# Convolution: 15 of the last 128 channels' 31 taps moved from TensorE to VectorE, between the levels of the RWKV inverse

## The chip, the cores and the metric

The program runs on one NeuronCore of a Trainium2 chip. The metric is the device time of one execution in microseconds. Kernels are compared by the median of their runs. TensorE (PE in the profile, its weight loads PEld), VectorE (DVE), ScalarE (ACT), GpSimd (POOL) and SyncE (SP) each work through an instruction list of their own and meet at semaphores.

## The reference

A token block of 256 rows and 1024 columns goes through three layers in float32: a mixer of a convolution and an RWKV recurrence, cross attention and a gated feed-forward; then block attention, a Mamba-2 mixer, and four more gated feed-forwards. The change is in the first mixer:

```python
def conformer_conv(u, conv_w, conv_b, ln_g, ln_b):
    h = u[..., :D_CONV] * jax.nn.sigmoid(u[..., D_CONV:])
    h = lax.conv_general_dilated(
        h, conv_w[:, None, :], window_strides=(1,), padding=[(CONV_WIDTH - 1, 0)],
        dimension_numbers=("NWC", "WIO", "NWC"), feature_group_count=D_CONV) + conv_b
    h = layer_norm(h, ln_g, ln_b)
    return jax.nn.silu(h)
```

`CONV_WIDTH` is 31 and `D_CONV` is 512: each of 512 channels is a causal convolution of its own over 256 tokens. Beside it stands `rwkv7_recurrence`, a scan over tokens for 8 heads of 64, which the kernel computes in chunks of 64 tokens, with the inverse of a unit triangular matrix for each.

## The kernel before

Most of the kernel is a stream of weights: a 1 MB slot comes by DMA, ScalarE rounds it (`w_hi`), VectorE takes the rest (`w_lo`), and TensorE multiplies with both parts. Slots are numbered; `raw_weights` holds three.

Between the 11 slots of the input projection and those of the output projection stands the part that the change touches. Channels lie on partitions, 128 at a time (`c` = 0 to 3), tokens along the free dimension.

The convolution on TensorE. Four copies of the gated input `glu`, shifted by 0 to 3 tokens, come back from a scratch tensor into `shifted[c]`, and the taps come in `tap_rows`, which lies in slots of `raw_weights` that wait for `conv_mm` before they take weights again. One group (`c`, `g`) is four products of 32 channels each, for taps 4g to 4g+3, accumulated in PSUM bank `CONV_BANK`. So there are 32 groups; a group is 4 float32 products in the program and 8 MATMUL records in the profile (L865). `conv_taps(spot)` issues `IN_SPOT[spot]` groups at one of 13 places among the products of the inverse. ScalarE brings each pair of channel blocks out of PSUM with the bias (`conv_out`, L1583) and counts `conv_evac`; TensorE waits for 2 of it and transposes the result (`conv_to_tokens`, L875), for VectorE's layer norm.

The inverse. It is built for two token blocks t = 0, 1 in five levels `lv`. In a level TensorE does, for each t, the product Q (32 records of L849), which ScalarE copies out (L1599); then, for each t, XT and X (32 records each), which VectorE adds in (L2346, L2349), and the next level's Q of that t waits for the first of these. VectorE also masks the next level's left factors (`next_offsets`, L2335). The order on TensorE from level 1 on is: Q(0), Q(1), taps, XT(0), X(0), taps, XT(1), X(1), and then the next level. In level 4 it is: Q(0), Q(1), taps of spot 11, XT(0), `conv_to_tokens`, XT(1), with no X.

The order of all instructions is written out by hand for each engine. The names `late` and `late_taps` are new with the change; `tmp`, whose first 256 columns `late` takes, is idle between the normalisation of kk and the layer norm.

Of the kernel before, what the change touches and what calls it, by code (L numbers as in the profile page):

```python
# [10 lines left out]
ALU = mybir.AluOpType  # L11
# [3 lines left out]
P = 128  # L15
T = 256
# [7 lines left out]
CONV_WIDTH = 31  # L24
# [16 lines left out]
for _name, _count in STREAM:  # L41
# [3 lines left out]


PCOLS = [("gain", 80), ("ssm_norm", 16), ("mu", 14), ("w0", 4), ("a0", 4), ("k_k", 4), ("k_a", 4), ("r_k", 4),
         ("lnx_g", 4), ("lnx_b", 4), ("conv_b", 4), ("ln_g", 4), ("ln_b", 4),
         ("sconv_w", 128), ("sconv_b", 32), ("wa_up", 512), ("g_up", 512), ("w_dt", 256)]

PROWS = [("q_gain", 128), ("k_gain", 128), ("dt_bias", 32), ("a_log", 32),
# [19 lines left out]
def build_program(nc, W, cols, rows, post_gains, consts, x_in, mem_in, pos_in, taps, edges, gated, out):  # L71
    with ExitStack() as ctx:
# [3 lines left out]
        def sem(name):  # L76
            return ctx.enter_context(nc.semaphore(name))
# [8 lines left out]
        tap_rows = [raw[:, 2 * q:2 * q + 2, :].rearrange("p h n -> p (h n)") for q in range(2)]  # L86
# [4 lines left out]
        shifted = [ap[:].bitcast(F32).rearrange("p (j t) -> p j t", j=4) for ap in (g_hi_t, g_lo_t)] \  # L91
# [22 lines left out]
        PS = ctx.enter_context(nc.psum_tensor("PS", [P, 8, 512], F32))  # L114

        def pc(name, i=0, n=1):
            at = PAT[name][0] + i
            return ptab[:, at:at + n]
# [5 lines left out]
        def cn(name, i=0, n=None):  # L124
            at, w = CAT[name]
            n = w if n is None else n
            return ctab[:, at + i:at + i + n]
# [16 lines left out]
        def region(at, words):  # L144
            assert at + words <= ARENA, (at, words)
            return arena[:, at:at + words]
# [9 lines left out]
        conv = region(o, 1024); o += 1024  # L156
        usig = conv
        MEM = region(o, 2048).rearrange("p (t d) -> p t d", t=TT)
        glu = region(o, 1024); o += 1024
# [25 lines left out]
        inv16 = c65(inv65)[:, :, 1:65]  # L185
        mem_squares = region(o - 1024, 2048).rearrange("p (t d) -> p t d", t=TT)
        tmp = region(o, 1024); o += 1024
        tmpb = V_t.rearrange("p t d -> p (t d)")
        CY = glu.rearrange("p (c t) -> p c t", c=4)

# [71 lines left out]
        S = namedtuple("Signals", NAMES)(*[sem(n) for n in NAMES])  # L262
# [4 lines left out]

            eng.wait_ge(S.half_done, LOOP * i + 2 * (FIRST[name] + slot) + 2)

        TAP_GROUPS = [(c, g) for c in range(4) for g in range(8)]  # L270
        IN_SPOT = [3, 2, 3, 3, 3, 2, 3, 3, 3, 3, 2, 2, 0]
        assert sum(IN_SPOT) == len(TAP_GROUPS) and 4 * 8 >= CONV_WIDTH
        CONV_BANK = 4
        X_BANKS = (5, 7)
# [6 lines left out]
        def half_cols(ap, lv, s):  # L281

            return ap.rearrange("p (b s w) -> p b s w", s=2, w=2 << lv)[:, :, s, :]

        def pair_cols(ap, lv):

            return ap.rearrange("p (e b s w) -> p e b s w", e=2, s=2, w=2 << lv)[:, :, :, 1, :]

        def pair_banks(t, lv):

            return PS[:, 2 * t:2 * t + 2, 0:256].rearrange("p e (b s w) -> p e b s w", s=2, w=2 << lv)[:, :, :, 1, :]
# [222 lines left out]
        def _(pe):  # L514
# [235 lines left out]
            for n in range(11):  # L750
# [5 lines left out]
                if n == 2:  # L756
# [3 lines left out]
                    for q, rows_ in enumerate((slice(0, 64), slice(64, 128))):  # L760
                        for c in range(4):
                            at = PAT["wa_up"][0] + c * P
# [3 lines left out]
                if n == 4:  # L766

                    pe.wait_ge(S.a_ready, 1)
                    for c in range(4):
                        last = mm(PS[:, 6 + c // 2, c % 2 * T:(c % 2 + 1) * T], pc("g_up", c * P, P), Q[:, 13, :],  # L770
                                  start=True, stop=True)
                    last.then_inc(S.g_done, 1)
                    pe.wait_ge(S.kksq_ready, 1)
                    for c in range(4):
                        last = mm(PS[32 * c:32 * c + 32, 4, 0:T], cn("pair32"), tmp[:, c * T:(c + 1) * T], start=True,
                                  stop=True)
# [77 lines left out]
            def conv_taps(spot):  # L854

                first = sum(IN_SPOT[:spot])
                for c, g in TAP_GROUPS[first:first + IN_SPOT[spot]]:
                    if c % 2 == 0 and g == 0:
                        pe.wait_ge(S.shifts_loaded, 8 * 16 * (c // 2 + 1))
                        pe.wait_ge(S.aside_loaded, 16 * (c // 2 + 2))  # L860
                        if c:
                            pe.wait_ge(S.conv_evac, 1)
                    for j in range(4):
                        at = ((c % 2 * 8 + g) * 4 + j) * 32
                        last = mm(PS[32 * j:32 * j + 32, CONV_BANK, c % 2 * T + 4 * g:(c % 2 + 1) * T],  # L865
                                  tap_rows[c // 2][:, at:at + 32], shifted[c][:, j, 0:T - 4 * g], start=g == 0, stop=g == 7)
                    if c % 2 and g == 7:
                        last.then_inc(S.conv_mm, 1)

            def conv_to_tokens():  # L870

                pe.wait_ge(S.conv_evac, 2)
                for t in range(TT):
                    for c in range(4):
                        last = nc.tensor.transpose(PS[:, CONV_IN_BANKS[t], c * P:(c + 1) * P],  # L875
                                                   conv[:, c * T + t * P:c * T + (t + 1) * P], ident)
                last.then_inc(S.convT_done, 1)
# [15 lines left out]
            pe.wait_ge(S.tok_ready, 4)  # L893
            grams_of_k_and_r(0)
            conv_taps(0)
            conv_taps(1)
            pe.wait_ge(S.gram_ready, 2)
            grams_of_a(1)
            conv_taps(2)
            grams_of_k_and_r(1)  # L900

# [47 lines left out]
            def state_kv(t):  # L949
                for c, cs in enumerate(pairs):  # L950
                    for g in range(2 * t, min(2 * t + 2, NCK - 1)):
                        mm(PS[:, 4 + g, cs], K_t[half(g), t, cs], V_t[half(g), t, cs], start=c == 0, stop=False)
# [60 lines left out]
                        if c == 3:  # L1013
                            last.then_inc(S.yc_done, 1)

            pe.wait_ge(S.conv_evac, 2)
            state_kv(0)
            pe.wait_ge(S.rounded_ready, 1)
            pe.wait_ge(S.u_ready, 1)
# [28 lines left out]
            for c in range(4):  # L1048
                for t in range(TT):
                    at = c % 2 * T + t * P  # L1050
# [285 lines left out]
            for n in range(8):  # L1336
# [5 lines left out]
                for j in range(2):  # L1342
                    c = (2 * n + j) % KC
# [8 lines left out]
        def _(act):  # L1352
# [163 lines left out]
            for n in range(11):  # L1516
                split(min(2 * n + 4, 23))
                done(act, "w_in", n)
                if n in MIXED:
                    for j in range(2):  # L1520
                        c = MIXED[n] + j
                        last = A(Q[:, c, :], PS[:, n % 4, j * T:(j + 1) * T], ACT.Copy, scale=mu_rest[:, c:c + 1])
                    last.then_inc(S.pin_ready, 1)
                elif n in VALUE_SLOTS:
                    q = VALUE_SLOTS.index(n)
                    A(glu[:, q * 512:(q + 1) * 512], PS[:, n % 4, :], ACT.Copy).then_inc(S.pin_ready, 1)
                else:
                    q = GATE_SLOTS.index(n)
# [50 lines left out]
            def conv_out(q):  # L1579

                act.wait_ge(S.conv_mm, q + 1)
                for c in (2 * q, 2 * q + 1):
                    last = A(conv[:, c * T:(c + 1) * T], PS[:, CONV_BANK, c % 2 * T:(c % 2 + 1) * T], ACT.Identity,  # L1583
                             bias=pc("conv_b", c))
                last.then_inc(S.conv_evac, 1)
# [10 lines left out]
            for lv in range(5):  # L1596
                for t in range(TT):
                    act.wait_ge(S.invq_done, 2 * lv + t + 1)
                    A(pair_cols(Qis[t], lv), pair_banks(t, lv), ACT.Copy).then_inc(S.invq_ready, 1)  # L1599
                    if t and lv < TT:  # L1600
                        act.wait_ge(S.ru_done, lv + 1)
                        A(RU0[:, lv, :], PS[:, 6, :], ACT.Copy).then_inc(S.ru_ready, 1)
                for t in range(TT):
                    if (lv, t) == (1, 0):
                        conv_out(0)
                    if lv < 3:
                        act.wait_ge(S.invx_done, 2 * (2 * lv + t) + 2)
                        q_zeroed(lv + 1, t)
            conv_out(1)
            for t in range(TT):  # L1610
                act.wait_ge(S.u_done, t + 1)
# [112 lines left out]
            for s in range(16):  # L1724
# [5 lines left out]
                ks = slice(s * P, (s + 1) * P)  # L1730
# [73 lines left out]
            for n in range(16):  # L1804
# [3 lines left out]
                for j in range(2):  # L1808
                    c = 2 * n + j
# [144 lines left out]
        def _(dve):  # L1954
            v = nc.vector
            steps = [0]

            def step(ins):

                steps[0] += 1  # L1960
                ins.then_inc(S.dve_step, 1)
                dve.wait_ge(S.dve_step, steps[0])
# [326 lines left out]
            def plus_eye(ap):  # L2289

                return v.tensor_tensor(h8(ap), h8(ap), b8(cn("eye64")), ALU.add)
# [37 lines left out]
            plus_eye(Xis[0]).then_inc(S.inv_ready, 1)  # L2329
            dve.wait_ge(S.gram_ready, 6)  # L2330
            plus_eye(Xis[1]).then_inc(S.inv_ready, 1)
            def next_offsets(lv, t):

                dve.wait_ge(S.invq_done, 2 * lv + t + 1)
                v.tensor_tensor(h8(Loffs[t]), h8(NLs[t]), b8(cn("off", (lv + 2) * 64, 64)), ALU.mult)  # L2335

            for lv in range(4):
                if lv:
                    for t in range(TT):
                        next_offsets(lv, t)  # L2340
                for t in range(TT):
                    if lv == 0:
                        next_offsets(lv, t)
                    dve.wait_ge(S.invx_done, 2 * (2 * lv + t) + 1)
                    part = pair_cols(XiTs[t], lv)
                    v.tensor_tensor(part, part, pair_banks(t, lv), ALU.add).then_inc(S.inv_ready, 1)  # L2346
                    dve.wait_ge(S.invx_done, 2 * (2 * lv + t) + 2)
                    part = half_cols(Xis[t], lv, 0)
                    v.tensor_tensor(part, part, half_cols(PS[:, X_BANKS[t], :], lv, 0), ALU.add).then_inc(S.inv_ready, 1)  # L2349
            for t in range(TT):  # L2350
                dve.wait_ge(S.invx_done, 16 + t + 1)
                part = pair_cols(XiTs[t], 4)
                v.tensor_tensor(part, part, pair_banks(t, 4), ALU.add).then_inc(S.inv_ready, 1)
# [522 lines left out]
```

## Time and profile before

| | before |
|---|---|
| median of 3 runs | 1570.42 us |
| lowest, highest | 1568.79, 1571.0 us |
| the profiled execution | 1571.65 us |
| its span | 1569.6 us |
| its mean granted TensorE clock | 0.999 |
| PE busy, PEld busy | 1544.0 us, 1345.6 us |
| DVE busy, ACT busy | 1101.8 us, 828.9 us |

The span goes from the first to the last instruction of the profile; the time has 2.05 us more around it. A busy PE counts overlapping products once. In the chain, a row "issue" is time in which TensorE had nothing to do and waited for no semaphore or transfer that the profile shows.

### The profile page before, as it was taken

To read this page: it belongs to the slowest core of one execution; us is meant where nothing else is said; L and a number is where in the kernel's file an instruction comes from. 1 tells how busy PE (TensorE), PEld (TensorE's weight loads), DVE (VectorE), ACT (ScalarE), POOL (GpSimd) and SP (SyncE) were. 2 spreads that over 40 slices of the span, in tenths; PEclk is the share of its full clock that TensorE was granted. 3 is DMA by queue.
4 is the path that set the end of the run, shared out by engine and by line. 5 is a ranking of instruction groups with operands and counts; after the bars stand their busy time and mean duration, and the time that the engine had idled before them with its cause. 6 is when DMAs were issued, how large, how long until landed. Compare 5 with 4: busy or idle time off the path is not lost.

```text
span 1569.6 us, 26683 instructions
## 1 busy us (share of the span) xinstructions
PE 1544.0 (98%) x10644; PEld 1345.6 (86%) x10644; DVE 1101.8 (70%) x1379; ACT 828.9 (53%) x1238; POOL 56.1 (4%) x69
## 2 busy tenths in 40 slices
PE   9999999999999999999999999999999998999999
PEld 8977899888888888888888888888889986788887
DVE  4865955776678767677776767766779938576765
ACT  7633755544446444467644446444466659454443
POOL 1000000000000000000000000000001036000000
PEclk9999999999999999999999999999999999999999
DMA  8332543555554545543455454555534540445452
GB/s 304 139 93 84 178 174 123 187 186 199 187 187 162 194 181 191 205 166 135 138 208 190 179 195 167 187 207 189 181 141 165 187 186 29 164 177 195 178 196 107
DMA packets 41156, 268.46 MB, mean 171 GB/s; under 512 B 5232, under 2 KB 8048, under 8 KB 9712
## 3 DMA queue, kind: packets, MB, share of 16 engines
q1 hardware_dynamic: 40368, 264.63, 46.8%
q0 software_dynamic: 704, 2.62, 0.5%
q8 instruction: 63, 1.03, 0.3%
q14 instruction: 21, 0.17, 0.0%
HBM read 265.66 MB, written 1.58 MB: 170 GB/s over the span
## 4 chain that ended last, share of the span: by engine, by line
PE 92%; DVE 3%; ACT 2%; DMA 1%; issue 1%; SPq 0%; DVEq 0%; ACTq 0%
PE PS L633 25%; PE PS L565 15%; PE PS L566 15%; PE PS L567 15%; PE PS L636 13%; PE PS L849 1%; DMA raw_weights<-W 1%; PE PS L865 1%; PE PS L648 1%; PE PS L655 1%; PE PS L649 1%; PE PS L521 1%; DVE w_lo L1971 1%; ACT x_normed L1874 0%; PE PS L733 0%
## 5 line engine op out<-in xcount | busy, mean ns | idle before, releaser
L1971 DVE TENSOR_TENSOR w_lo<-raw_weights,w_hi 128x1024 fp32r<-128x1024 f32 x487 | 590.0, 1229 | 330.9 <-ACT w_hi L1366 329.6
L1366 ACT ACTIVATE w_hi<-raw_weights 128x1024 fp32r<-128x1024 f32 x488 | 506.4, 1055 | 279.0 <-PE PS L567 135.0
L633 PE MATMUL PS<-h_both,w_hi 128*128 128x512 f32 x1680 | 419.9, 392 | 0.0
L633 PEld LDWEIGHTS PS<-h_both,w_hi 128*128 128x128 f32 x1680 | 304.9, 189 | 56.5
L636 PEld LDWEIGHTS PS<-h_both,w_lo 128*128 128x128 f32 x1680 | 229.2, 190 | 16.4
L636 PE MATMUL PS<-h_both,w_lo 128*128 128x256 f32 x1680 | 234.3, 282 | 0.0
L565 PE MATMUL PS<-w_hi,g_hi 128*128 128x512 f32 x440 | 171.8, 390 | 0.0
L566 PE MATMUL PS<-w_lo,g_hi 128*128 128x512 f32 x440 | 171.8, 390 | 0.0
L567 PE MATMUL PS<-w_hi,g_lo 128*128 128x512 f32 x440 | 171.2, 389 | 0.0
L565 PE MATMUL PS<-h_both,w_hi 128*128 128x256 f32 x560 | 161.0, 288 | 2.6 <-DVE h_both L1997 1.4
L566 PE MATMUL PS<-h_both,w_hi 128*128 128x256 f32 x560 | 158.4, 283 | 0.0
L567 PE MATMUL PS<-h_both,w_lo 128*128 128x256 f32 x560 | 158.3, 283 | 0.0
L565 PE MATMUL PS<-w_hi,h_both 128*128 128x512 f32 x352 | 139.9, 397 | 1.7 <-DVE h_both L2749 1.1
L567 PE MATMUL PS<-w_hi,h_both 128*128 128x512 f32 x352 | 137.7, 391 | 0.0
L566 PE MATMUL PS<-w_lo,h_both 128*128 128x512 f32 x352 | 137.6, 391 | 0.0
L1462 ACT ACTIVATE silu_gate<-silu_gate 128x512 f32<-128x512 f32 x55 | 34.7, 632 | 188.8 <-DVE silu_gate L2126 188.8
L565 PEld LDWEIGHTS PS<-h_both,w_hi 128*128 128x128 f32 x560 | 107.1, 191 | 5.8 <-DVE w_lo L1971 3.3
L566 PEld LDWEIGHTS PS<-h_both,w_hi 128*128 128x128 f32 x560 | 107.2, 192 | 0.4 <-issue 0.2
L567 PEld LDWEIGHTS PS<-h_both,w_lo 128*128 128x128 f32 x560 | 107.2, 191 | 0.0
L567 PEld LDWEIGHTS PS<-w_hi,g_lo 128*128 128x128 f32 x440 | 82.6, 188 | 17.6
L565 PEld LDWEIGHTS PS<-w_hi,g_hi 128*128 128x128 f32 x440 | 82.8, 188 | 15.9
L566 PEld LDWEIGHTS PS<-w_lo,g_hi 128*128 128x128 f32 x440 | 82.8, 188 | 15.3
(401 smaller groups left out, 1598.2 us busy)
## 6 DMA issues: line engine op xcount, KB each, us to landing
raw_weights<-W SPq DMA_DIRECT2D x243, 1024.0 KB, 4.8
raw_weights<-taps SPq DMA_DIRECT2D x2, 1024.0 KB, 5.8
post_gain<-post_gains POOLq DMA_DIRECT2D x3, 512.0 KB, 3.9
x_resid<-x SPq DMA_DIRECT2D x2, 512.0 KB, 4.1
raw_weights<-W SPq DMA_DIRECT2D x2, 512.0 KB, 7.1
h_both<-gated SPq DMA_DIRECT2D x8, 128.0 KB, 3.0
arena<-mem POOLq DMA_DIRECT2D x1, 1024.0 KB, 5.5
out<-x_resid SPq DMA_DIRECT2D x2, 512.0 KB, 2.7
```

The source lines that it names most:

```text
L521: return nc.tensor.transpose(PS[:, xT_base(k) + c // 2, at:at + P], X[:, t, c * P:(c + 1) * P], ident)
L565: mm(out, lhs[0], rhs[0], start=start, stop=False)
L566: mm(out, lhs[0], rhs[1], start=False, stop=False)
L567: return mm(out, lhs[1], rhs[0], start=False, stop=stop)
L633: mm(both_out, w_hi[:, slot, c * P:(c + 1) * P], h_both[:, :, c, :], start=c == 0, stop=False)
L636: last = mm(PS[:, bank + j, 0:T], w_lo[:, slot, c * P:(c + 1) * P], h_hi[:, c, :], start=False, stop=c == KC - 1)
L648: mm(PS[:, bank + j, 0:T], w_lo[:, (n + j) % H, cs], h_hi[:, c, :], start=c == 0, stop=False)
L649: mm(PS[:, bank + j, 0:T], w_hi[:, (n + j) % H, cs], h_hi[:, c, :], start=False, stop=c == KC - 1)
L655: last = mm(PS[:, bank + j, T:2 * T], w_hi[:, (n + j) % H, cs], h_lo[:, c, :], start=c == 0, stop=c == KC - 1)
L1366: A(w_hi[:, n % H, :], raw[:, n % (2 * R), :], ACT.Copy).then_inc(S.hi_ready, 1)
L1462: A(sg[:, b % 2, :], sg[:, b % 2, :], ACT.Silu).then_inc(S.silu_ready, 1)
L1971: v.tensor_tensor(w_lo[:, n % H, :], raw[:, n % (2 * R), :], w_hi[:, n % H, :].bitcast(F32), ALU.subtract).then_inc(S.lo_ready, 1)
```

## The change

Channel block c = 3 has 4 groups on TensorE (taps 0 to 15) in place of 8. Taps 16 to 30 are 15 instructions on VectorE, each multiplying `glu` by one tap's weight and adding it to `late`, four after each of the levels 0 to 2 and three after level 3. Each of them waits for the one before (`step`). At the end `late_joined` adds PSUM, bias and `late` on VectorE in two instructions; ScalarE brings out only c = 2 in its second `conv_out`, and the transposes wait for `conv_evac` 3. The 15 columns of weights are added to the table `ptab`.

```diff
-        TAP_GROUPS = [(c, g) for c in range(4) for g in range(8)]
-        IN_SPOT = [3, 2, 3, 3, 3, 2, 3, 3, 3, 3, 2, 2, 0]
+        GROUPS_OF = [8, 8, 8, 4]
+        TAP_GROUPS = [(c, g) for c in range(4) for g in range(GROUPS_OF[c])]
+        IN_SPOT = [3, 2, 3, 3, 3, 2, 2, 2, 2, 2, 2, 2, 0]
...
-                for c in (2 * q, 2 * q + 1):
+                for c in (0, 1) if q == 0 else (2,):
                     last = A(conv[:, c * T:(c + 1) * T], PS[:, CONV_BANK, c % 2 * T:(c % 2 + 1) * T], ACT.Identity,
...
+            def late_taps(ks):
+
+                for k in ks:
+                    weight = pc("late_taps", k - 16)
+                    x = glu[:, 3 * T:4 * T - k]
+                    if k == 16:
+                        dve.wait_ge(S.glu_ready, 2)
+                        step(v.tensor_scalar(late[:, k:T], x, weight, None, ALU.mult))
+                    else:
+                        step(v.scalar_tensor_tensor(late[:, k:T], x, weight, late[:, k:T], ALU.mult, ALU.add))
+
+            def late_joined():
+
+                dve.wait_ge(S.conv_mm, 2)
+                dve.wait_ge(S.conv_evac, 2)
+                v.tensor_scalar(conv[:, 3 * T:3 * T + 16], PS[:, CONV_BANK, T:T + 16], pc("conv_b", 3), None, ALU.add)
+                v.scalar_tensor_tensor(conv[:, 3 * T + 16:4 * T], PS[:, CONV_BANK, T + 16:2 * T], pc("conv_b", 3),
+                                       late[:, 16:T], ALU.add, ALU.add).then_inc(S.conv_evac, 1)
...
                     v.tensor_tensor(part, part, half_cols(PS[:, X_BANKS[t], :], lv, 0), ALU.add).then_inc(S.inv_ready, 1)
+                late_taps(range(16 + 4 * lv, min(20 + 4 * lv, CONV_WIDTH)))
+            late_joined()
```

On TensorE, before, the stretch from level 2's second spot of taps (spot 8) to the transposes; a program row of `x32` is twice as many records in the profile, the last number is the count:

```order
L865 MATMUL PS<-h_both,raw_weights 32x256 x4
L849 MATMUL PS<-arena 64x8x4 x32
L849 MATMUL PS<-arena,silu_gate 64x2x16 x16
L849 MATMUL PS<-arena 64x2x16 x16
L865 MATMUL PS<-h_both,raw_weights 32x252 x4
L865 MATMUL PS<-h_both,raw_weights 32x248 x4
L865 MATMUL PS<-h_both,raw_weights 32x244 x4
L849 MATMUL PS<-silu_gate,arena 64x2x16 x16
L849 MATMUL PS<-arena,silu_gate 64x2x16 x16
```

The same stretch with the change (line numbers are two higher):

```order
L867 MATMUL PS<-h_both,raw_weights 32x236 x4
L851 MATMUL PS<-arena 64x8x4 x32
L851 MATMUL PS<-arena,silu_gate 64x2x16 x16
L851 MATMUL PS<-arena 64x2x16 x16
L867 MATMUL PS<-h_both,raw_weights 32x232 x4
L867 MATMUL PS<-h_both,raw_weights 32x228 x4
L851 MATMUL PS<-silu_gate,arena 64x2x16 x16
L851 MATMUL PS<-arena,silu_gate 64x2x16 x16
```

The spot between Q and XT has two groups where it had three. The same holds for spots 6, 7 and 8, and the spots after them keep their two groups, which are now the last of c = 3 sooner in its tap order.

On VectorE, with the change, from the last addition of level 2 to the transposed inverse's last additions; all `L2343` rows, `L2349` and `L2350` are new:

```order
L2343 SCALAR_TENSOR_TENSOR arena<-arena,ptab 128x229
L2356 TENSOR_TENSOR silu_gate<-arena,ctab 128x512
L2356 TENSOR_TENSOR arena<-arena,ctab 128x512
L2367 TENSOR_TENSOR arena<-arena,PS 128x16x16
L2370 TENSOR_TENSOR arena<-arena,PS 128x16x16
L2343 SCALAR_TENSOR_TENSOR arena<-arena,ptab 128x228
L2343 SCALAR_TENSOR_TENSOR arena<-arena,ptab 128x227
L2343 SCALAR_TENSOR_TENSOR arena<-arena,ptab 128x226
L2349 TENSOR_SCALAR arena<-PS,ptab 128x16
L2350 SCALAR_TENSOR_TENSOR arena<-PS,ptab,arena 128x240
L2376 TENSOR_TENSOR arena<-arena,PS 128x8x32 x2
```

So the taps stand ahead of the masks of the next level, and the join stands ahead of the additions of level 4.

## Rows read from the trace of the kernel before

**Rows 1.** The page: busy time of two engines, and the chain by engine.

```profile
PE 1544.0 (98%) x10644; PEld 1345.6 (86%) x10644; DVE 1101.8 (70%) x1379; ACT 828.9 (53%) x1238; POOL 56.1 (4%) x69
...
PE 92%; DVE 3%; ACT 2%; DMA 1%; issue 1%; SPq 0%; DVEq 0%; ACTq 0%
```

**Rows 2.** The chain by time, 101 to 136 us: start, length, what.

```profile
101.21 0.96 issue
...
105.57 0.42 issue
...
109.75 0.08 issue
...
112.30 1.57 PE PS L849 x63
113.87 1.41 PE PS L865 x24
115.28 1.92 PE PS L849 x89
117.20 0.00 issue
...
119.34 1.52 PE PS L849 x64
...
121.17 0.14 issue
121.31 1.41 PE PS L865 x22
122.72 2.10 PE PS L849 x104
124.83 0.32 issue
...
128.61 0.94 PE PS L865 x16
129.55 2.45 PE PS L849 x127
132.00 1.08 issue
...
133.27 0.96 PE PS L865 x16
...
134.25 0.85 ACT arena L1583 x2
...
135.24 1.06 PE PS L875 x8
```

**Rows 3.** DMA queues, 99 to 134 us: packets, MB, share.

```profile
q8 instruction: 9, 0.15, 1.9%
```

**Rows 4.** VectorE's timeline at level 2: start, length, instruction, idle before it.

```profile
116.85 0.42 DVE L2349 TENSOR_TENSOR arena<-arena,PS 128x256 f32<-128x256 f32 x1 [0.48 <-PE PS L849]
117.58 0.69 DVE L2335 TENSOR_TENSOR silu_gate<-arena,ctab 128x512 f32<-128x512 f32 x1 [0.30 <-PE PS L849]
118.19 0.68 DVE L2335 TENSOR_TENSOR arena<-arena,ctab 128x512 f32<-128x512 f32 x1
120.00 0.42 DVE L2346 TENSOR_TENSOR arena<-arena,PS 128x256 f32<-128x256 f32 x1 [1.13 <-PE PS L849]
```

**Rows 5.** VectorE groups by form: count, busy us, mean ns, idle.

```profile
L2661 DVE SCALAR_TENSOR_TENSOR x_normed<-PS,ptab,x_normed 128x254 f32<-128x254 f32 x32 | 15.4, 481 | 1.1
...
L2569 DVE TENSOR_SCALAR arena<-arena,small 128x256 f32<-128x256 f32 x8 | 2.8, 348 | 0.0
...
L2223 DVE SCALAR_TENSOR_TENSOR arena<-arena,ptab 128x256 f32<-128x256 f32 x4 | 1.7, 482 | 0.0
...
L2642 DVE TENSOR_SCALAR small<-PS 128x64 f32<-128x64 f32 x1 | 0.2, 216 | 0.0
```

More of the change, by code:

```diff
@@ L47 @@
 PCOLS = [("gain", 80), ("ssm_norm", 16), ("mu", 14), ("w0", 4), ("a0", 4), ("k_k", 4), ("k_a", 4), ("r_k", 4),
-         ("lnx_g", 4), ("lnx_b", 4), ("conv_b", 4), ("ln_g", 4), ("ln_b", 4),
+         ("lnx_g", 4), ("lnx_b", 4), ("conv_b", 4), ("ln_g", 4), ("ln_b", 4), ("late_taps", CONV_WIDTH - 16),
          ("sconv_w", 128), ("sconv_b", 32), ("wa_up", 512), ("g_up", 512), ("w_dt", 256)]
@@ L187, in build_program @@
         tmp = region(o, 1024); o += 1024
+        late = tmp[:, 0:T]
         tmpb = V_t.rearrange("p t d -> p (t d)")
@@ L865, in conv_taps @@
                         last = mm(PS[32 * j:32 * j + 32, CONV_BANK, c % 2 * T + 4 * g:(c % 2 + 1) * T],
-                                  tap_rows[c // 2][:, at:at + 32], shifted[c][:, j, 0:T - 4 * g], start=g == 0, stop=g == 7)
-                    if c % 2 and g == 7:
+                                  tap_rows[c // 2][:, at:at + 32], shifted[c][:, j, 0:T - 4 * g], start=g == 0, stop=g == GROUPS_OF[c] - 1)
+                    if c % 2 and g == GROUPS_OF[c] - 1:
                         last.then_inc(S.conv_mm, 1)
             def conv_to_tokens():
-                pe.wait_ge(S.conv_evac, 2)
+                pe.wait_ge(S.conv_evac, 3)
                 for t in range(TT):
@@ L1014, in rows_carried @@
                             last.then_inc(S.yc_done, 1)
-            pe.wait_ge(S.conv_evac, 2)
+            pe.wait_ge(S.conv_evac, 3)
             state_kv(0)
@@ L2856 @@
               "conv_b": col(a["conv_b"][0]), "ln_g": col(a["conv_ln_g"][0]),
-              "ln_b": col(a["conv_ln_b"][0]), "sconv_w": col(a["ssm_conv_w_2"][0].reshape(-1)),
+              "ln_b": col(a["conv_ln_b"][0]), "late_taps": a["conv_w"][0][::-1][16:, 3 * P:].T, "sconv_w": col(a["ssm_conv_w_2"][0].reshape(-1)),
               "sconv_b": col(a["ssm_conv_b_2"][0]), "wa_up": wa, "g_up": a["g_up"][0], "w_dt": wdt}
```

## The prediction

> **What bounds the kernel now.** I read three views in this order: the page for the bound, the chain by time for this stage, then VectorE's timeline for room. The page says TensorE: busy 98% of the span, 92% of the chain [rows 1]. So a microsecond taken from TensorE's list is worth up to a microsecond, and VectorE's work is free as long as nobody waits for it.
>
> In the stage of the change the chain is products and taps, L849 and L865, back to back, but it has holes called "issue" at 101.21, 105.57, 109.75, 117.20 (0.00), 121.17, 124.83 and 132.00 us [rows 2]. The reader should measure from the end of one hole to the end of the next. 102.17, 105.99, 109.83: 3.82 and 3.84 us. 117.20, 121.31, 125.15: 4.11 and 3.84. 125.15 to 133.08 is 7.93, twice 3.97; 109.83 to 117.20 is 7.37, twice 3.69. And between the holes at 121.17 and 124.83 stand 22 + 104 = 126 records of products [rows 2], each with its weight load. In the same 35 us an instruction queue moves 9 packets of 0.15 MB in all, one each 3.9 us [rows 3]. I read this as instruction fetch: about every 128 products a new block of code is needed, and in this stage TensorE runs through its small products as fast as the blocks come.
>
> The Trainium skill ("Runtime: NRT & Kernel Launch", Instruction fetch mechanics) says that an engine's code is refilled in blocks of 16 KiB, 256 instructions, and that crossing a boundary is mostly hidden. The trace agrees on the block (128 products and 128 loads, 0.15 MB over 9 packets) and not on the second point, as the hole of 1.08 us shows. By the page alone no hole comes back; that is a rival below.
>
> **The change part by part.**
>
> *Four groups fewer.* Sixteen records of taps take 0.94 us and 24 take 1.41 [rows 2], so a group of 8 is 0.47 us, and four are 1.88 us. Without the fetch that would be the gain. But a group is only 8 of the 128 products of a block: where the fetch ends the wait, it is worth 8/128 of 3.83 us, or 0.24 us, and four are worth 0.96 us. Which one holds is to be walked through.
>
> I take these lengths from [rows 2]: two groups 0.94; XT and X of one t with the next two Q, 128 records, 2.45 to 2.5; XT and X of the other, 1.52; and a block no shorter than 3.83 us, the commonest distance. From 113.87 to the boundary at 117.20 are 24 + 89 = 113 records, so the boundary before lies some 14 products ahead of 113.87, at 113.5. All this is an estimate from those rows.
> Spot 6 now ends at 113.87 + 0.94 = 114.81. The next boundary is 98 products into the 128 that follow, reached at 116.7, but the code is there only at 113.5 + 3.83 = 117.3. The other 30 take until 117.9. Spot 7, 1.52 us of products and spot 8 end at 117.9 + 0.94 + 1.52 + 0.94 = 121.3, 126 products on: the boundary, with no wait (117.3 + 3.83 = 121.2). The 128 small products that follow need 2.5 us, but their block is followed by the next at 121.3 + 3.83 = 125.1: a hole of 1.3 us. Then spot 9, 1.52 and spot 10 end at 128.5; the 128 products, with a boundary 32 into them at 129.1 and no wait, end at 131.0, and spot 11 at 131.97. Before, spot 11 ended at 133.27 + 0.96 = 134.23. The last taps are 2.26 us earlier. The next boundary is then some 14 products into XT(0), with its code at 129.1 + 3.83 = 132.97; 18 products are left, so XT(0) ends at 133.35.
> In the kernel before, the hole of 1.08 us at 132.00 stood ahead of spot 11 and thus ahead of ScalarE's and TensorE's last steps of the convolution. Now such a hole falls behind the taps, where TensorE has to wait for the convolution anyway. So the two waits lie over each other.
>
> *The join.* ScalarE's two evictions took 0.85 us and the transposes came 0.14 us after [rows 2]. Now one takes about 0.46, then VectorE does 16 columns and 240 columns. No row has a 16-column one; it costs at most the 0.216 us of 64 columns [rows 5], and at least nothing; I take 0.15, near the row, since 16 columns can't save much against 64. The second is 0.48, after the 128x254 form from PSUM [rows 5]. With 0.05 for the semaphore between: 131.97 + 0.02 + 0.46 + 0.05 + 0.15 + 0.48 + 0.14 = 133.27. Alone the join is some 0.3 us longer than before; here it is done as XT(0) ends at 133.35, so I charge nothing. The transposes start at about 133.35 instead of 135.24: 1.9 us earlier. If the cover were gone, the 0.3 us would count.
>
> *Fifteen taps on VectorE.* The first is a multiplication of 240 columns, about 0.35 us; the others are like the 0.482 us of the 256-column one in SBUF [rows 5]. Waiting for the one before, which adds some 0.03, four make about 2.0 us, all together 7.2 us. They stand ahead of the masks. In level 2 before, VectorE ended an addition at 117.27, did the masks by 118.87 and was idle 1.13 us until 120.00 [rows 4]. In the walk above X(1) of level 1 ends at about 116.1, its addition at 116.5, the taps at 118.5, the masks at 119.8, and the additions of XT(0) and X(0) at 120.2 and 120.6. The next Q(0) waits for the first of these; TensorE reaches it after 64 of the 128 products from 121.3, at 122.5. The slack is 2.3 us. XT(1)'s addition comes after 121.9, when VectorE is free. After level 3 only three taps are left, 1.5 us from about 130.7; they end at 132.2, before the join may start at 132.5. So VectorE's taps cost nothing; the cover is TensorE's 64 products and a spot of taps. Queued behind them on VectorE are the masks and additions, and behind `late_joined` the additions of level 4, wanted by TensorE only after the transposes and XT(1).
>
> *The rest.* Fifteen more columns of `ptab` come with a transfer at the start, in the shade of weights: nothing. Weight slots start 2.3 us sooner as `conv_mm` does: nothing, since an earlier load makes nobody wait. TensorE is busy 98% of the span [rows 1], past this stage as in it, so the gain stays. A shift of the code by 64 instructions may put a small hole in or out elsewhere; I take nothing, and 0.4 us either way.
>
> The sum: 1571.65 - 1.9 = 1569.75 us for the profiled execution. This one stood 1.23 us over the median of the runs, 1570.42, so the median should be 1568.5 us. The bounds hang on the length of a block. With 3.69 us (the 7.37 for two) the walk gives a gain of some 2.4 us; with the 4.11 of the longest every block waits, the last boundary comes at 134.0 and the gain is 0.85 us.
>
> **The rivals.**
> *No hole comes back.* If the holes are no rule but leftovers, 1.88 us of taps go and with them 0.14 + 0.32 + 1.08 = 1.54 us of holes, less 0.3 for the join: 3.1 us, 1567.3 us. For it speaks that 117.20 has length 0.00; against it the even distances. The page of the Trainium skill named above, which calls the crossing mostly hidden, would have it so.
> *The fetch takes all.* Blocks of over 4 us, as the one of 4.11 and the two of 3.97, and the join bare on the path: a gain of 0.85 less 0.3, about 0.5 us, 1569.9 us. For it: two of four late distances are that long. Against it: in those TensorE also had 24-record spots to do, so the fetch may not have been what it waited for.
> *Slower, by VectorE.* The dependent taps delay the addition that Q(0) waits for. The slack is 2.3 us over four taps; so a tap would have to cost over 0.5 + 0.6 = 1.1 us, more than twice the row of 0.482. At 2 us a tap the three inner levels lose 3.6 us each, some 11 in all, less the 1.9: 1579 us. No row of a VectorE instruction of this size comes near; 1 in 20 or less.
> *The change doesn't do what it says* is hardly open: the four groups are gone from the list; only their worth is in question.
>
> **How the numbers follow.** The forecast (gain 1 to 3 us) has 0.68, the first rival 0.14, the second 0.13, the third and unknown losses 0.05. The range of 1566.3 to 1570.6 leaves out the slower case and part of the first rival's tail; the bounds 0.85 and 2.4 lie within, with about 1 us for the medians, as the runs before spread over 2.2 us. A measurement of this kernel can tell about 0.2%, 3.1 us, from no change. Faster than that needs the first rival or more: 0.16. Slower: 0.05. Within: 0.79.
>
> **What would show it.** Right: the transposes start near 133.4 us; the holes again at distances of 3.8 us, one of over 1 us behind level 3's two Q and ahead of spot 9, one inside XT(0) of level 4; VectorE's taps at 0.49 us from start to start, and no TensorE wait for its additions. Wrong: holes gone or of other distances; TensorE waiting for L2367; the transposes waiting for the join long after XT(0). The prediction as a whole fails if later stages lose what this one gains, or if the clock falls in the thinner stretch.

## The result: slower by 0.2%

| | before | with the change |
|---|---|---|
| median | 1570.42 us (21 runs) | 1573.5 us (21 runs) |
| ratio to before, 95% interval | | 1.002 (1.0014 to 1.0026) |
| the profiled execution | 1571.65 us | 1572.06 us |
| its span, mean granted clock | 1569.6 us, 0.999 | 1569.9 us, 0.999 |

The forecast was 1568.5 us and the range ended at 1570.6. The time went the other way, by 3.1 us. One of the 21 executions of before took 2544.14 us; without it the median is the same. The two profiled executions lie only 0.4 us apart, since the one of before was 1.2 us over its median and the one with the change 1.4 us under its own.

The chain by time of the changed kernel (start, length, what), as [rows 2] of before; every line number is two higher up to the join:

```profile
109.45 0.89 PE PS L830 x30
110.34 0.91 PE PS L867 x16
111.26 1.16 PE PS L851 x50
112.42 0.36 issue
...
116.41 0.61 issue
...
121.11 2.45 PE PS L851 x128
123.56 0.38 issue
...
130.04 1.01 PE PS L867 x16
131.05 0.02 issue
131.08 0.48 ACT arena L1585
...
131.69 0.23 DVE arena L2349
131.92 0.39 DVE arena L2350
132.31 0.14 issue
132.44 1.07 PE PS L877 x8
133.51 0.60 PE PS L851 x32
134.11 2.11 PE PS L830 x70
136.22 3.02 issue
139.23 1.96 PE PS L830 x58
...
149.10 1.43 DVE arena L2402 x4
...
150.57 1.43 PE PS L1002 x41
```

Read it in two halves. Up to the transposes (L877) it is better than the forecast: they start at 132.44 us, where the walk had 133.35 and before 135.24 [rows 2]. 0.47 us of that is a head start from the first 20 us of the execution. Then, 3.8 us after the transposes have started, TensorE stops in the middle of 128 like products of L830, behind the 70th, and does nothing for 3.02 us, with no semaphore in sight. From the transposes to L1002 it takes 18.13 us, before 15.08 (150.32 less 135.24). The other 1400 us are as before, within 0.1 us.

What stands there is on the DMA queues. SyncE's timeline of the changed kernel shows when the three weight slots behind the convolution are issued, as its last taps end:

```profile
131.07 1.28 SPq L464 DMA_DIRECT2D raw_weights<-W  x3
```

In the view of DMA queues the changed kernel has no code packet (q8) from 130.3 to 136.5 us, while 1.64 MB of weights move; the next comes in 136.5 to 138 us:

```profile
q1 hardware_dynamic: 216, 1.64, 73.6%
...
q1 hardware_dynamic: 89, 0.61, 97.9%
q8 instruction: 1, 0.02, 4.0%
```

The packets came 3.3 to 4.1 us apart until 129.2 us, so one was due near 133, and the first weights moved at 132.0. In the kernel before, that packet is in the window from 134 to 135.1 us and no weights are yet:

```profile
q8 instruction: 1, 0.02, 5.3%
```

Its slots are issued at 134.25:

```profile
134.25 2.17 SPq L462 DMA_DIRECT2D raw_weights<-W  x3
```

The packet moves at 134.4 us and the first weights at 135.2. There the code won by less than a microsecond; with the change the last taps end some 3 us sooner, the boundary of the code lies 64 instructions further on in the work, and the transfers win. So far this is a reading of two traces; the experiments test it.

### The profile page after: what moved, and what is told of

The parts are those of the page before. It is cut to its first block, busy times and chain, and to the rows that moved or that the text cites. A ratio compares the mean times of both kernels' runs of the same rounds, so it can differ in the third digit from the quotient of the medians.

```text
span 1569.9 us, 26639 instructions
## 1 busy us (share of the span) xinstructions
PE 1542.3 (98%) x10612; PEld 1344.9 (86%) x10612; DVE 1108.7 (71%) x1396; ACT 828.2 (53%) x1237; POOL 55.9 (4%) x69
## 4 chain that ended last, share of the span: by engine, by line
PE 92%; DVE 3%; ACT 2%; issue 1%; DMA 1%; SPq 0%; DVEq 0%; ACTq 0%
PE PS L635 25%; PE PS L567 15%; PE PS L568 15%; PE PS L569 15%; PE PS L638 13%; PE PS L851 1%; DMA raw_weights<-W 1%; PE PS L650 1%; PE PS L867 1%; PE PS L657 1%; PE PS L651 1%; PE PS L523 1%; DVE w_lo L1973 1%; ACT x_normed L1876 0%; PE PS L735 0%
## 5 line engine op out<-in xcount | busy, mean ns | idle before, releaser
L1368 ACT ACTIVATE w_hi<-raw_weights 128x1024 fp32r<-128x1024 f32 x488 | 506.4, 1055 | 278.9 <-PE PS L569 135.1
```

What stands on the lines that cost most here:

```text
L1368: A(w_hi[:, n % H, :], raw[:, n % (2 * R), :], ACT.Copy).then_inc(S.hi_ready, 1)
```

## The experiments

All times are medians beside the kernel before on the same chip.

| run | time | before | ratio (95%) |
|---|---|---|---|
| e1_hold | 1568.68 | 1569.76 | 0.9991 (0.9982 to 0.9999) |
| e2_one_first | 1569.71 | 1569.76 | 0.9999 (0.9991 to 1.0008) |
| e3_after_shifted | 1573.26 | 1569.76 | 1.0017 (1.0008 to 1.0026) |
| e4_before_shifted | 1589.82 | 1569.76 | 1.013 (1.0115 to 1.0144) |
| e5_after_mid64 | 1572.46 | 1569.91 | 1.0011 (1.0001 to 1.002) |
| e6_before_mid192 | 1581.64 | 1569.91 | 1.0076 (1.006 to 1.0093) |
| e7_before_hold | 1568.74 | 1569.91 | 0.9996 (0.9986 to 1.0005) |
| e8_after_again | 1572.86 | 1569.91 | 1.002 (1.001 to 1.0029) |
| e9_after_hold | 1569.36 | 1570.7 | 0.9991 (0.9982 to 1.0) |
| e10_before_hold | 1569.78 | 1570.7 | 0.999 (0.9981 to 0.9999) |
| e11_hold_one_tap | 1568.83 | 1570.7 | 0.999 (0.9981 to 0.9999) |
| e12_hold_groups_only | 1569.58 | 1570.7 | 0.9986 (0.9977 to 0.9995) |
| e13_narrow_taps | 1572.61 | 1569.87 | 1.0022 (1.0008 to 1.0037) |
| e14_few_groups | 1567.22 | 1569.87 | 0.9983 (0.9973 to 0.9992) |
| e15_after_spread | 1576.9 | 1569.87 | 1.0054 (1.0039 to 1.0069) |
| e16_before_spread | 1573.38 | 1569.87 | 1.0024 (1.0014 to 1.0033) |

### The transfers held back

```diff
             sp.wait_ge(S.conv_mm, 2)
+            sp.wait_ge(S.convT_done, 1)
             slot_in(12)
             slot_in(13)
             slot_in(14)
```

> The changed kernel, with the three weight slots behind the convolution held until the transposes of the convolution are done (about 1.5 us later). Theory A (the 3.02 us hole at 136.22 us is a fetch of TensorE's code, wanted at about 133 us, that stands behind the three 1 MB transfers begun at 132.04): the fetch starts before the transfers and that hole is gone or under 0.5 us; but the fetch after it, wanted about 137.5 us, now falls among the transfers, so a later hole of 0 to 3 us may come near 141 us; median 1570 to 1572. Theory B (VectorE's 15 taps and the join cost the time, the hole is only where it shows): the hole or an equal one stays at the same place, median 1573.5 as the changed kernel.

1568.68 us. By the ratios to before (0.9991 and 1.002) that is 4.6 us under the changed kernel, and the hole is gone. The chain of e1_hold at the same place:

```profile
123.33 1.20 issue
...
132.88 1.06 PE PS L878 x8
133.94 0.60 PE PS L852 x32
134.54 3.79 PE PS L831 x128
```

The 128 products that were 70 and 58 around a hole are one piece of 3.79 us. Nothing of VectorE's taps or of the join was touched, so theory B falls. The later hole that I allowed for did not come.

The slots are issued at 134.01 us in its trace, some 2.5 us after the last taps.

Half of the cure, one slot first and two later (`sp.wait_ge(S.z_done, 1)` ahead of `slot_in(13)`):

> The changed kernel, but of the three weight slots only the first starts at the end of the taps, the other two once the first state product is done (about 143 us). Theory A: the fetch wanted at about 133 us stands behind 1 MB (under 3 us) and starts by about 134.5, the hole at 136.2 shrinks from 3.0 to under 1.2 us, median 1569.5 to 1571.5. Theory B: 1573.5 and the hole as before.

1569.71 us, and the hole at the same product shrinks to 1.65 us, more than the 1.2 I had allowed, with 1 MB ahead of the code in place of 3:

```profile
133.18 2.11 PE PS L831 x70
135.28 1.65 issue
136.93 1.96 PE PS L831 x58
```

### The code boundaries moved

Products were added that do nothing but fill the list. In e3 and e4 they stand in the warm-up, 16 of them in e3, and in e4 52 with four long ones fewer:

```diff
-            keep_busy(8)
+            keep_busy(4)
+            for _ in range(52):
+                mm(PS[:, 3, 0:8], eps.broadcast_to([P, P]), eps.broadcast_to([P, 8]), start=True, stop=True)
```

> The changed kernel with 16 tiny products (32 products and 32 loads, 64 instructions) more in TensorE's warm-up, which puts each later code boundary where it was in the kernel before. Theory A: the fetch that met the transfers is asked for some 0.7 us sooner, before them; the hole of 3 us at 136 us is gone, and the gain of 1.9 to 2.3 us shows: median 1568 to 1569.5 (up to 1 us more if the warm-up is on the path). Theory B: 1573.5 or slower.

> The kernel before, with nothing of the change, but with 192 instructions more in TensorE's warm-up (and four of its eight long products fewer), which moves the code boundaries behind to where a kernel with 64 instructions fewer has them: one falls behind the last taps. Theory A: the kernel before gets a hole of 2 to 3.5 us at 138 to 140 us, at the same place among the products of L828, and is 1 to 4 us slower: 1571.5 to 1574.5. Theory B: 1570.4, no such hole.

Both times lie above what I gave, and both are spoiled by the place: with the thin products at the start the granted clock is half for 6.8 us in e3 and for 20.5 us in e4 in the profiled executions, where before and the change have it full in their first 30 us. The traces still answer: e3's hole at L830's products (L832 in its listing) is gone, and e4, the kernel before, has one of 2.47 us at them, behind the 70th. So the padding was put behind the input projection:

```diff
             pe.wait_ge(S.g_ready, 1)
+            for _ in range(48):
+                mm(PS[0:64, 6, 0:32], ident[0:64, 0:64], ident[0:64, 0:32], start=True, stop=True)
```

(48 in the kernel before, 16 in the changed one).

> The changed kernel with 16 small products (64 instructions, at most 1 us) more ahead of the stage, after the input projection, so that the warm-up of the clock is as it was and only the code boundaries move back to where the kernel before has them. Theory A (fetch behind the transfers): no hole of 2 us or more at the products of L828/L830, median 1569.3 to 1571 with the small products' own 0.8 us in it. Theory B (VectorE's taps and join): 1574.

> The kernel before with 48 small products (192 instructions, about 2.4 us of TensorE's time) more ahead of the stage; the code boundaries in the stage and after it fall as in the changed kernel. Theory A: a hole of 2 to 3.5 us among the products of L828 some 5 us behind the last taps, in some runs a fall of the clock behind it, median 1574.5 to 1577.5. Theory B: only the products' own time, 1572.8.

e5 has no such hole. Its median is above what I gave, since the padding took more than I thought: the stage begins at 91.74 us in its trace, 89.40 before, 2.3 us later. Less that it is 1570.1 us, the time of before. e6 is the plainest run of the study. It is the kernel before, with all its taps on TensorE and none on VectorE. Its chain:

```profile
142.75 2.11 PE PS L830 x70
144.85 2.44 issue
147.29 3.39 PE PS L830 x58
```

The hole is behind the 70th product, as in the changed kernel, and here too the view of DMA queues has no code packet while the weights begin to move: none from 139 to 144 us, the next between 144.4 and 145.5. And the 58 products after it take 3.39 us where they took 1.96. The view by stretches shows why (length; PE, PEld, DVE, ACT, POOL busy; granted clock; DMA share; GB/s):

```profile
144.80:147.20 2.40, 0.06 (x1) 0.00 (x0) 0.13 (x1) 2.37 (x4) 0.00 (x0) 0.97 1.01 416
147.20:150.60 3.40, 3.31 (x58) 3.25 (x58) 0.69 (x1) 2.76 (x3) 0.00 (x0) 0.52 0.59 246
```

After the idle 2.4 us the granted clock is half, 1.2 GHz, for 3.4 us, which costs 1.4 us more. e4 has the same behind its hole: 58 products in 3.28 us, and a clock of 0.53. e6 took 4.1 us more than the top of what I gave; a further half-speed stretch, of 6.8 us from 89.0 us, lies over its padding.

> The changed kernel again, for a second profile and more times. If the hole of 3 us brings the clock down in some executions, this one or its times show it: theory A expects times of two kinds, near 1571 to 1572 with one half-speed stretch of the clock and near 1574 with two. Theory B expects one kind.

1572.86 us against 1569.91, the first result over again, with a hole of 2.47 us behind the 70th product. The clock did not fall after it in this profile either. Among the 21 first runs of the changed kernel the 13 with a mean clock of 0.998 or less have a median of 1573.8 us and the 8 with 0.999 one of 1572.25. That does not show falls behind the hole: the kernel before divides the same way on the chip of e8 (8 runs at 0.998 or less with 1571.15 us, 17 above with 1569.72), and e9's profile has a stretch at half clock at 1146 us, far from this stage. Two clean kinds of times, as I had expected, don't show. How often the clock falls behind the hole of the changed kernel stays open; neither of its two profiles has it.

### What the change is worth with the collision away

> The kernel before with the three weight slots held until the transposes of the convolution are done, 2.5 us later than now. Its fetch at 134.4 us already goes ahead of the transfers, so theory A expects little: the fetch at 141.5 us may come later or sooner by up to 2 us; median 1569 to 1571. It is the base for the changed kernel with the same hold: what stands between the two is the change's own worth.

> The changed kernel with the slots held, again, now on the same chip as its base e10. Theory C (the stage runs at the pace of the code fetch, and a group of taps is worth 16 of 256 instructions): 0.3 to 1.3 us faster than e10. The recorded walk: 1.9 us faster. Theory B (VectorE's part costs what TensorE saves): equal to e10 or slower.

> The kernel before with the slots held, again: the base for the other three, 1568 to 1569.5.

> The changed kernel with the slots held and 14 of VectorE's 15 taps left out (the first and the join stay; taps 17 to 30 of the last 128 channels are then missing from the result). Theory C: VectorE's taps are hidden, the time is that of e9 within 0.6 us. Theory B: faster than e9 by 1 us or more.

> The kernel before with the slots held and the four groups simply left out, with nothing on VectorE and both evictions on ScalarE (taps 16 to 30 of the last 128 channels are missing from the result). It is the most that the change can bring. Theory C: 0.5 to 1.5 us faster than e10, since the fetch sets the pace. The price by taps alone: 1.9 us faster.

e11 left out all of VectorE's taps but the first (`if k > 16: continue`); e12 took `GROUPS_OF` and `IN_SPOT` of the change into e7, with the stop flag at the new last group, and nothing else. On one chip: 1569.78 with the groups (e10), 1569.58 without them and with nothing in their place (e12), 1569.36 with VectorE's taps (e9), 1568.83 with one of those (e11). The intervals of the four lie over each other, and the means of the same runs give another order: under e10 they are 0.1 us (e9), 0.5 (e11) and 0.9 (e12). So by the medians VectorE's taps cost 0.5 us and four groups are worth 0.2 to 0.9 us, and neither is told from nothing. The whole change, e9 under e10, is 0.1 us by the means and 0.4 by the medians, not the 1.9 forecast; e12 alone would not rule out 1.9 for the groups.

The held kernel before shows where my 1.9 came from. The hold acts only behind the transposes; ahead of them e7 is the kernel before, and yet its holes are small and its transposes are 3.1 us earlier than in the profile that I had:

The chain of e7_before_hold:

```profile
101.10 0.21 issue
...
104.72 0.27 issue
...
122.76 0.27 issue
...
129.89 0.10 issue
...
132.14 1.06 PE PS L876 x8
```

From the first product of the stage to the transposes the profiles of kernels with all groups have 45.84 (before), 42.72 (e7), 43.26 (e4), 42.88 (e6) and 44.50 us (e10), with a mean of 43.8; those of the changed one 43.51, 44.13 (e8), 43.34 (e1), 41.80 (e2), 43.61 (e3), 44.24 (e5) and 42.81 (e9), with a mean of 43.35. Left out are the kernels below, whose taps or transfers in this stage are others. I had walked from the slowest of five.

### Columns or instructions

```diff
-                        last = mm(PS[32 * j:32 * j + 32, CONV_BANK, c % 2 * T + 4 * g:(c % 2 + 1) * T],
-                                  tap_rows[c // 2][:, at:at + 32], shifted[c][:, j, 0:T - 4 * g], start=g == 0, stop=g == 7)
+                        n = 8 if g else T
+                        last = mm(PS[32 * j:32 * j + 32, CONV_BANK, c % 2 * T + 4 * g:c % 2 * T + 4 * g + n],
+                                  tap_rows[c // 2][:, at:at + 32], shifted[c][:, j, 0:n], start=g == 0, stop=g == 7)
```

> The kernel before with the slots held, and 28 of the 32 groups of taps with 8 columns in place of 228 to 252 (most of the convolution is missing from the result); the instructions are as many as before. Theory C (code fetch sets the pace): the stage's code still comes at one block in 3.5 to 3.8 us, so of the 7 to 8 us of columns saved in TensorE's work only 1 to 3 us show, and the holes called issue grow by the rest: median 1566.5 to 1568.5. If TensorE's columns set the pace: 7 to 8 us faster, 1562.

The chain of e13_narrow_taps, ahead of 114 us at the full clock and behind it not:

```profile
100.03 1.42 issue
...
104.48 0.80 issue
105.29 0.31 PE PS L850 x4
105.59 0.30 PE PS L867 x24
105.90 2.10 PE PS L850 x99
108.00 1.13 issue
...
112.08 1.04 issue
...
114.38 4.09 PE PS L850 x128
...
122.83 4.41 PE PS L850 x128
```

The spot of 24 tap records takes 0.30 us where it took 1.4. The holes take all of it back: they end at 101.45, 105.28, 109.13 and 113.12, 3.83, 3.85 and 3.99 us apart, much as in the kernel before [rows 2]. The block of code does not come sooner when TensorE has less to do. That is shown here with the same instructions and hardly any columns. Then the clock falls, and the same 128 products take 4.09 and 4.41 us, not 2.45:

In the view by stretches, with the columns as above:

```profile
120.00:135.00 15.00, 15.00 (x416) 13.94 (x412) 4.75 (x10) 1.99 (x5) 0.00 (x0) 0.50 0.01 3
```

So less work on TensorE made the kernel 2.7 us slower. By these rows it is about 10 us less (28 groups, 0.37 us each), not the 7 to 8 that I gave. I had not expected a fall of the clock. But the fall is not the whole answer: the three executions with the highest mean clock, 0.996 and 0.997, took 1570.1 to 1570.63 us, no less than the kernel before either.

```diff
+        GROUPS_OF = [8, 8, 1, 1]
+        IN_SPOT = [3, 2, 3, 3, 3, 2, 0, 0, 1, 0, 0, 1, 0]
```

> The kernel before with the slots held, and 14 of the 16 groups of the last two channel blocks left out (their taps 4 to 30 are missing from the result): 224 instructions fewer, 6.6 us of taps. Theory C: 224/256 of a block of 3.6 to 3.8 us, 3.1 to 3.4 us faster, and up to 1 us more or less by where the boundaries fall. If TensorE's columns set the pace: 6.6 us less what waits for the evictions between Q and XT that the taps no longer cover.

1567.22 us: 2.6 us under the unheld kernel before on its chip, and some 1.6 under the held one, if that stands 0.9 to 1.2 under as on the two other chips. 14 groups gave less than 0.2 us each; by taps they are 0.47 each, and by the block 0.24. So this is also half of the 3.1 to 3.4 us that I gave under the held kernel. Part of what is missing is in its trace: a hole of 0.79 us at 136.61, behind the transposes, while weights move, which e7 does not have. And its holes in the stage end 3.83, 3.44, 3.35 and 3.62 us apart (from 113.37 to 127.61), so the block has no fixed price.

### The transfers spread

```diff
+            slot_in(14)
             sp.wait_ge(S.half_done, 22)
             shifted_in(1)
+            sp.wait_ge(S.conv_mm, 1)
+            slot_in(12)
             sp.wait_ge(S.conv_mm, 2)
-            slot_in(12)
+            sp.wait_ge(S.convT_done, 1)
             slot_in(13)
-            slot_in(14)
```

> The changed kernel with its three weight slots spread: the third ahead of the stage (its place in raw_weights holds no taps), the first once the first two channel blocks are done (about 111 us), and only the second held until the transposes. Theory A: a fetch near 112 us may stand behind 1 MB (a hole up to 1.5 us there), none near 136; median 1568 to 1570. If it is 1567 or less, the collision was still in the held kernel.

> The kernel before with the same spreading: the base for e15. Theory C: e15 faster by 0.3 to 1.3 us; by the recorded walk 1.9 us.

Both are worse than before. e15 lies above what I gave, and it is 3.5 us slower than its base e16, where I had it faster by 0.3 to 1.3. It looks like the same mechanism at another place. In e15 the slot sent once the first two channel blocks are done (113.28 us) has its 1 MB moving from 114.2 us, and the next code packet moves only at 117.7; the chain of e15:

```profile
115.77 2.04 PE PS L853 x97
117.80 2.24 issue
120.05 1.07 PE PS L853 x31
121.12 1.80 PE PS L869 x16
```

The 16 tap records after the hole take 1.80 us in place of 0.94, with the clock at 0.51 from 119 to 133 us. e16 has a hole of 1.37 us at 118.72 and kept its clock in the profile. Both have one more hole, 1.55 us at 94.47 in e15 and 1.02 us at 94.75 in e16, behind the slot that is sent ahead of the stage; no other run separates that one. In this kernel it did not help to send transfers where the queue was empty, since code was being fetched there.

## Why the prediction was wrong

**The step that failed** is in "The rest" of the prediction: "Weight slots start 2.3 us sooner as `conv_mm` does: nothing, since an earlier load makes nobody wait." I had found that TensorE lives on its code fetch here, and had the fetch as a fixed 3.83 us a block, without asking what else uses the same DMA engines. The transfers start 3 us sooner in this stage, ahead of a code packet in place of behind it, and TensorE waits for that packet. It costs 2.5 to 3.0 us of hole (e8 and the first profile), and by e6 1.4 us more where the clock falls after it. Of the 4.6 us between the changed kernel and e1_hold this is the greater part; the rest I can't divide, since the hold alone also gave the kernel before 0.9 to 1.2 us by the medians (e7, e10; e7's interval allows nothing), for a cause that stays open. One that I only suppose is that its code, too, sometimes loses the race of 134 us. Of the 3.1 us by which the medians went the wrong way, the hole less the 0.5 us by which the changed kernels' stage is shorter in the mean makes 2.0 to 2.5; the remaining 0.6 to 1.1 us are not attributed.

**The gain of 1.9 us** was mis-sized. That the blocks set the pace is right (e13), and that a group counts with its instructions fits: by the block that is 0.96 us for four, and the medians give 0.2 to 0.9. The fixed 3.83 us is not right: in the changed kernel's first profile holes end at 112.78, 117.02 and 123.93, which is 4.24 us and twice 3.46. And my walk added what the holes of one execution happened to be. It took the end of the hole of 1.08 us ahead of the last taps as the change's gain, while another execution of the kernel before hardly has it (e7: 0.10 us). I had noted that the profiled execution stood 1.23 us over the median and only moved the sum by it.

**The shape of the walk** held: a hole behind level 3's two Q and ahead of spot 9 (1.3 us forecast; 0.38 in the first profile, 1.20 in e1). The hole inside XT(0) of level 4 is in e8, 0.54 us. In the first profile the 32 products of XT(0) take 1.01 us, which the wait for the join hides; in e1 they take 0.67, with no hole.

**The join** was sized right: 1.30 us from the last taps to the transposes forecast, 1.39 measured, with 0.48 for ScalarE, then 0.23 and 0.39 for VectorE, where I had 0.15 and 0.48: two errors that nearly cancel. That it would be hidden under XT(0) was not so in the first profile, where the transposes wait 0.50 us for it; in e8 XT(0) covers it, as forecast. **VectorE's taps** were right: four in 1.96 us (2.0 forecast), no TensorE wait for one of the inverse's additions, and e11 without them is not clearly faster.

**The rivals.** "The fetch takes all" was nearest for the worth of the groups. The slower rival that I gave, by VectorE, was the wrong mechanism, and 0.05 for all slower cases was far too little where the changed step releases 3 MB of transfers. The Trainium skill ("Runtime: NRT & Kernel Launch", Instruction fetch mechanics) calls the crossing of a code boundary mostly hidden; in this stage the measurement decides against it twice, by the holes of 0.80 to 1.42 us at the boundaries of e13 and by those of 2.4 to 3.0 us where transfers stand in the way.

## What to carry to other kernels

When TensorE waits for nothing that the profile shows, measure the distances between the ends of the waits and count instructions between them: if they are even, suspect that work is priced by instructions and not by columns, and test it as e13 does. Then treat the code fetch as one more transfer with a due time, and look at what bulk transfer a faster step releases into it; holding that transfer for 2.5 us was worth more here than the work removed. Take a stall from one execution as a draw, not as a term: a second profile of the kernel before would probably have shown this one to be a slow one.

## What the runs showed of the hardware

A code packet of 16 KB (0.02 MB in the rows) that was due near 133 us moved only after 136.5 us when 3 MB of weights were under way. The stop of TensorE came one block of products behind the hole before it (in e8 17, 8, 32 and 70 of them), and lasted 1.65 us with 1 MB ahead (e2) and 2.4 to 3.0 us with 3 MB. An idle 2.44 us of TensorE was followed by 3.4 us at half clock in e6 and 2.47 us by the same in e4, while 3.02 us in the first profile of the changed kernel and 2.47 us in e8 were not: the length of the hole alone does not tell. With the taps thinned to 8 columns the clock was half for 27 us in the middle of a busy kernel (e13, TensorE busy 15.00 of 15.00 us at 0.50); with the wide taps in their places (e7) it was 1.00 from 114 to 134 us.
